# Five moves in one decoder layer: prompt compression inside the projection, and three out-projection blocks inside sample attention

## The chip, the cores and the metric

The kernel runs on one core of a Trainium2 chip. Its engines are TensorE (PE, with weight loads shown apart as PEld), VectorE (DVE), ScalarE (ACT), GpSimd (POOL) and SyncE (SP); each works through its own list of instructions, and semaphores tie the lists together. The metric is the device time of one execution in microseconds, as the median of several runs.

## The reference, cut to what matters

One layer of a hybrid decoder, in float32, for a prompt (1 x 512 rows) and a sample group (8 x 4 = 32 rows) that share every weight. All 544 rows stand side by side in the kernel.

```python
mod = silu(c) @ w_ada + b_ada; shift, scale, gate = split(mod, 3)
h = rms_norm(x, norm_g) * (1 + scale) + shift
(a_q, a_kv, a_gate, a_silu, b_in, b_silu, c_q, c_kv, c_iq, c_ik, c_iw, c_silu) = split_columns(h @ w_in)
# group A: for the rows so far, chunks of 32 positions, one every 16, become one key and one value:
#   hid = b1 + sum over 32 positions of (chunk + pe) @ w1 ;  gelu(hid) @ w2 + b2
#   o_a = gated sum of attention over compressed, selected and window keys (8 heads, 2 key heads)
# group B: trailing means of b_in, times pool_w ; group C: attention over keys that an indexer selects
mixed = concat(o_a * silu(a_silu), o_b * silu(b_silu), o_c * silu(c_silu))      # 2048 columns
y = x + gate * (mixed @ w_out)
```

The sample group attends to 2048 cached positions per sequence, read through a page table; the prompt group only to itself. A T5 bias table is added to all scores.

## The kernel before

The work runs in stages, which the windows of the trace below name by their time.

**0 to 484 us:** the cached rows of the sample group are compressed (16 groups of 16 pages, `NPOS` = 16; `load_rows`, `round_rows`, `turn_hid`, `w2_mm`), and beside that `mod` is computed. **484 to 525 us:** DVE's `modulate()` applies scale and shift to the normalised rows `hT` (16 feature blocks of 512 prompt rows, then the sample rows), the last group of the compression is finished, ACT and DVE round `h` into a high and a low part (`h_hi`, `h_lo`), and the first small jobs of the input projection begin in native float32. **To 1206 us:** the input projection. From job `J0` on there are 32 jobs, one for each block of 128 columns (called `jj` 0 to 31 here); each is 16 blocks `k` of the features times two halves of 272 rows times three products (low x high, high x low, high x high), so 96 matmuls. SP loads each job's weights in two pieces (`hw_raw`, `x` = 2 jj and 2 jj + 1), ACT and DVE round them (`hw_hi`, `hw_lo`). Other work hangs in this loop: `sample_indexer(j, k)` on PE, `hook(j)` on several engines.

**1206 to 1254 us (called phase 2 here):** the prompt's own compression. After the projection's last `silu` columns DVE adds the position embedding to the prompt's chunks (`xpe`), PE multiplies 2 x 32 of them by `w1P` (8 MB, loaded from 1205.7 us on), ACT applies gelu, PE `w2P`, and the keys `kcP` and values `vcP` come out. SP also loads here the bias of the prompt's scores (`bias`, 3 MB) and the rows of `silu` (`mix`, 4.35 MB), in one transfer each. **To 1430 us:** prompt attention, 48 units of one head and 128 rows; `scores(u)` on DVE adds the bias, `gated(u)` multiplies by `mix`, which thereby becomes `mixed`.

**1430 to 1701 us:** sample attention, in the steps head 0, body 0, head 1, turn 0, body 1, head 2, turn 1, body 2, turn 2. The 112 key blocks are numbered through: units 0 and 1 are the two key heads of group A (blocks 0 to 39 and 40 to 79), unit 2 is group C (80 to 111); head 1 has blocks 40 to 47, body 1 blocks 48 to 79, head 2 blocks 80 to 87, body 2 blocks 88 to 111. A block is loaded into one of `NKR` = 8 buffers `kn` (SP issues the loads of two of every four blocks, ACT the others, and each of them waits until the block eight before has been turned), turned by four PE transposes into bank 5 or 6 (`kb`), copied out by ACT (`kT`), and multiplied with the queries for four blocks at a time (`kmm`). In the bodies of units 1 and 2 the products of the unit before with its values stand among the blocks (`pv(u - 1, 0)` to `pv(u - 1, 5)`; 6 stands behind the body, 7 at the next turn; even numbers are the products, odd ones a small sum). POOL loads the values (`vr`, `vx`) page by page, into buffers that a `pv` has set free. A turn transposes the softmax's result. **1701 to 1919 us:** the out projection, 16 column blocks `nb` of 96 matmuls each (16 `k` x 2 halves x 3 products), then `y_turn(nb)`, five transposes back to rows; DVE scales by the gate and adds `x`; SP loads `wo`, ACT and DVE round it.

`after(engine, n)` is a barrier: it waits until all engines have ended phase n. PE's transposes and products in `kb`, `pv` and phase 2 are native float32, which PE runs as two records for each matmul; the rounded products are one record each.

Of the kernel before, what the change touches and what calls it, by code (L numbers as in the profile page):

```python
# [38 lines left out]
P = 128  # L39
# [20 lines left out]
NXP = KVH * NCP + 1  # L60
# [129 lines left out]
def build(nc, I, O):  # L190
# [3 lines left out]
    with ExitStack() as ctx:  # L194
# [94 lines left out]
        iqT = ext("iqT", P, 2 * TT)  # L289
        ikT = ext("ikT", P, T)  # L290
# [24 lines left out]
        w1p, w1pos = region(tp[0])  # L315
        w1P = [w1p(f"w1P{i}", P, 32 * 256) for i in range(2)]
        w1_early = (big_end - tp[0]) // (16 * 256 * 4)
        w2p, _ = region(w1pos[0])
        xpe = w2p("xpe", P, 2 * 32 * NXP)
        w2P = w2p("w2P", P, 2 * 2 * P)  # L320
        hidP = w2p("hidP", P, 4 * 64)
        cxP = w2p("cxP", P, 3 * 64)
        hidr = [w2p(f"hidr{i}", P, 256) for i in range(2)]
        att, apos = region(tp[0])
        bias = att("bias", P, 12 * T)
        assert 12 * T <= 32 * 256
# [7 lines left out]
        keep, _ = region(apos[0] + 12 * 1024)  # L334
        kc = keep("kc", P, DB * KVH * P)
# [134 lines left out]
        cr_x, cr_ps, cr_ev = sem("cr_x"), sem("cr_ps"), sem("cr_ev")  # L470
# [40 lines left out]
        mx_in = sem("mx_in")  # L511
# [22 lines left out]
        y_out = sem("y_out")  # L534
        BIAS_BANKS = (1, 4, 7, 1, 4)
# [131 lines left out]
        kb_gt, g_ = {}, 32  # L667
        for step, u in STEPS:
            if step == "turn":
                g_ += len(pgroups(u))  # L670
            else:
                for n in blocks_of(step, u):
                    kb_gt[n] = g_
                    g_ += 1

        by_act = [True] * 32
        for step, u in STEPS:
            if step == "turn":
                by_act += [(len(by_act) + i) % 2 == 0 for i in range(len(pgroups(u)))]
            else:  # L680
                by_act += [True] * len(blocks_of(step, u))
# [19 lines left out]
        def block_pages(eng, regs, b, first, n):  # L701

            eng.load(regs[0:n], ptab[0:1, b * NPG + first:b * NPG + first + n])
            return [eng.snap(regs[i], min_val=0, max_val=NPOOL - 1) for i in range(n)]

# [47 lines left out]
        def after(eng, n):  # L753

            eng.wait_ge(ph_pe, n)
            eng.wait_ge(ph_act, n)
            eng.wait_ge(ph_dve, n)
            if n == 4:
                eng.wait_ge(ph_pool, 1)
# [186 lines left out]
        def _(sp):  # L946
# [14 lines left out]
            def load_rows(g, first, n):  # L961
                kv, b = g // DB, g % DB
                if g >= 2:
                    sp.wait_ge(xn_tr, 8 * (g - 1))
                for x in range(first, first + n):
                    t, i = x // 4, x % 4
                    r = page(b, x)
                    sp.dma_start(xnat[(4 * g + t) % 8][32 * i:32 * i + 32, :].rearrange("p (l x) -> p l x", l=4),
                                 ca[bass.ds(r, 1), :, kv, :, :].rearrange("a (p l) h c -> (a p) l (h c)", l=4)).then_inc(xn_in[g % 2], 16)
# [12 lines left out]
            load_rows(0, 0, NPG)  # L982
            for i in range(2, 4):
                load_w1(0, i)
# [32 lines left out]
            for x in range(2 * (njobs - J0)):  # L1017
# [15 lines left out]
            for i in range(4):  # L1033
                if i == w1_early:
                    after(sp, 2)
                    for kv in range(2):
                        sp.dma_start(w2P[:, kv * 256:kv * 256 + 256].rearrange("p (n d) -> p n d", n=2), I["a_cmp_w2"][0, kv].rearrange("(n p) d -> p n d", p=P)).then_inc(late_in, 16)
                kv, s0 = i // 2, i % 2 * 16
                sp.dma_start(w1P[kv][:, s0 * 256:(s0 + 16) * 256].rearrange("p (s h) -> p s h", h=256),
                             I["a_cmp_w1"][0, kv].rearrange("(s p) h -> p s h", p=P)[:, s0:s0 + 16]).then_inc(w1q_in[i], 16)  # L1040

            for x in range(2):
                sp.wait_ge(sx_out[x], 16 * KD // 2)
            sp.dma_start(mix[:, :], d_mix).then_inc(mx_in, 16)

            sp.wait_ge(cr_ps, 1)
            sp.wait_ge(b_dma, 32 + 64)
            sp.dma_start(v3(bias, "p (h j) -> p h j", h=12), bass.AP(d_rep.tensor, d_rep.offset + 127, [[12 * TXL - 1, P], [TXL, 12], [1, T]])).then_inc(at_in, 16)
            after(sp, 3)
# [8 lines left out]
            after(sp, 4)  # L1058
            sw = I["state_a_win"][0]

            def keys(step, u):
                for n in blocks_of(step, u):
                    if n >= NKR:
                        if n % 4 >= 2:
                            continue
                        sp.wait_ge(kb_tr, kb_gt[n - NKR] + 1)
                    key_block(sp, regs, n)
# [19 lines left out]
            for c in range(D // CW):  # L1087
# [7 lines left out]
                elif c == 0:  # L1095
                    after(sp, 5)
# [6 lines left out]
        def _(pool):  # L1103
# [127 lines left out]
            after(pool, 4)  # L1231
# [12 lines left out]
        def _(pe):  # L1244
# [266 lines left out]
            def sample_indexer(j, k):  # L1511

                jj = j - J0
                if (jj, k) == (0, 1):
                    pe.wait_ge(a_free, aux)
                    pe.wait_ge(ixp_r, 12)
                    mm(bank[5][:, 0:4], expd[:, 2 * P:3 * P], iwS[:, :], start=True, stop=True).then_inc(si_ps, 1)
# [11 lines left out]
                if (jj, k) == (9, 11):  # L1529
                    ix_sum(4)  # L1530

# [18 lines left out]
            for j, (kind, b, t, c) in enumerate(jobs):  # L1550
                if free_need[j]:
                    pe.wait_ge(m_free, free_need[j])
                if j >= J0:
                    for k in range(KD):
# [5 lines left out]
                        sample_indexer(j, k)  # L1560
                        wh, wl = (v3(t_[x % 4], "p (k n) -> p k n", n=P)[:, k % 8, :] for t_ in (hw_hi, hw_lo))
# [14 lines left out]
                if c == SMALL:  # L1576
                    if j == 0:
                        pe.wait_ge(hw_in[0], in_need[0])
                    for k in range(KD):
                        if j == 0:  # L1580
                            pe.wait_ge(h_ready, k + 1)
                        if (j, k) == (0, 8):
                            turn_hid(15)
                        if (j, k) == (1, 8):
# [41 lines left out]
            pe.wait_ge(m_free, njobs)  # L1626
            for u in range(2):
                last = mm(bank[4][:, 24 * u:24 * u + 24], expd[:, u * P:(u + 1) * P], gateS0[:, :], start=True, stop=True)
            last.then_inc(pl_t, 1)
# [3 lines left out]
            after(pe, 2)  # L1633
            def turn_hidden(kv):
                pe.wait_ge(cr_ev, kv + 1)
                for hb in range(2):
                    tr(bank[2 + kv][:, 64 * hb:64 * hb + NXP], hidr[kv][0:NXP, hb * P:(hb + 1) * P], con[0:NXP, 0:NXP]).then_inc(cp_ps, 1)

            for kv in range(2):
                pe.wait_ge(cr_x, kv + 1)  # L1640
                for s in range(32):
                    if s % 16 == 0:
                        pe.wait_ge(w1q_in[2 * kv + s // 16], 48 + 16 * (2 * kv + s // 16 == 1))
                    last = mm(bank[kv][0:NXP, 0:256], xpe[:, (32 * kv + s) * NXP:(32 * kv + s + 1) * NXP], w1P[kv][:, s * 256:(s + 1) * 256],
                              start=(s == 0), stop=(s == 31))
                last.then_inc(cr_ps, 1)
            turn_hidden(0)
            turn_hidden(1)
            pe.wait_ge(late_in, 80)
            pe.wait_ge(cp_ev, 4)  # L1650
            for hb in range(2):
                last = mm(bank[4][:, 0:62], w2P[:, hb * P:(hb + 1) * P], hidP[:, hb * 64:hb * 64 + 62], start=(hb == 0), stop=(hb == 1))
            last.then_inc(cp_ps, 1)
            for h in range(KVH):
                for hb in range(2):
# [1229 lines left out]
```

## Time and profile before

| | us |
|---|---|
| median of 3 runs (smallest to largest) | 1922.06 (1920.43 to 1925.61) |
| the profiled execution | 1920.71 |
| its span | 1919.0 |
| PE busy (of the span) | 1731.9 (90%) |
| DVE busy | 1091.5 (57%) |
| ACT busy | 656.7 (34%) |

The chain that ended last runs through PE for 74% of the span; DVE has 7%, DMA 6%, SP's queue 5%. PE is the engine that sets the time in most stages, but not in all: in phase 2 and in sample attention it is idle for long stretches, which the windows below show.

### The profile page before, as it was taken

How to read it: one execution, taken by the hardware profiler on the slowest of the kernel's cores; microseconds unless marked ns; L12 is line 12 of the kernel's file. 1: busy time of each engine (PE TensorE's matmuls, PEld its weight loads, DVE VectorE, ACT ScalarE, POOL GpSimd, SP SyncE). 2: the span in 40 equal slices, each digit the busy share in tenths (PEclk: the TensorE clock that was granted, in tenths of full speed). 3: DMA queues.
4: the chain of work that ended last, by engine and by line, in shares of the span. 5: the costliest groups of instructions: out<-in, count | busy, mean ns of one | idle time of the engine just before them, and what ended most of it. 6: DMA issues, size and time to landing. Idle time of an engine off the chain costs nothing.

```text
span 1919.0 us, 34926 instructions
## 1 busy us (share of the span) xinstructions
PE 1731.9 (90%) x13423; PEld 1515.2 (79%) x13423; DVE 1091.5 (57%) x2145; ACT 656.7 (34%) x1339; POOL 224.2 (12%) x412
## 2 busy tenths in 40 slices
PE   5999989999799999999999999889976677769997
PEld 3788878989698888888999999567753444569997
DVE  4656685556434656344877746458765786343331
ACT  4555575555422312233222221044433333231110
POOL 1000000000001001432000000100012053710000
PEclk9999999999799989999999999859997788779999
DMA  9978868995323131655333332930018598753331
GB/s 237 259 209 229 242 175 232 288 261 167 89 72 107 62 106 45 174 176 171 106 83 83 102 90 68 320 122 2 1 58 259 165 289 243 215 181 96 119 123 47
DMA packets 275441, 291.39 MB, mean 152 GB/s; under 512 B 33093, under 2 KB 235318, under 8 KB 273597
## 3 DMA queue, kind: packets, MB, share of 16 engines
q1 hardware_dynamic: 233409, 210.82, 38.6%
q0 software_dynamic: 20000, 62.03, 9.8%
q10 hardware_dynamic: 21866, 16.30, 3.0%
q8 instruction: 107, 1.75, 0.4%
q14 instruction: 59, 0.48, 0.1%
HBM read 272.74 MB, written 29.14 MB: 157 GB/s over the span
## 4 chain that ended last, share of the span: by engine, by line
PE 74%; DVE 7%; DMA 6%; SPq 5%; issue 4%; ACT 3%; ACTq 1%; POOL 0%; POOLq 0%; DVEq 0%
PE bank L1564 6%; PE bank L1566 6%; PE bank L1565 6%; PE bank L1357 4%; PE bank L1356 4%; PE bank L1358 4%; PE bank L1898 3%; PE bank L1900 3%; PE bank L1899 3%; PE bank L1608 3%; PE bank L1609 3%; PE bank L1610 3%; PE bank L1334 3%; PE bank L1307 2%; DMA kn<-in_cache_a_kv_dram 2%
## 5 line engine op out<-in xcount | busy, mean ns | idle before, releaser
L1564 PE MATMUL bank<-h_lo,hw_hi 128*128 128x272 f32 x1024 | 305.2, 298 | 0.9 <-DVE hw_lo L2506 0.9
L1566 PE MATMUL bank<-h_hi,hw_hi 128*128 128x272 f32 x1024 | 296.7, 290 | 0.0
L1565 PE MATMUL bank<-h_hi,hw_lo 128*128 128x272 f32 x1024 | 295.3, 288 | 0.0
L1356 PE MATMUL bank<-w1hi,xl 128*128 128x256 f32 x768 | 225.5, 294 | 6.0 <-DVE w1lo L2332 3.8
L1357 PE MATMUL bank<-w1lo,xh 128*128 128x256 f32 x768 | 217.5, 283 | 0.0
L1358 PE MATMUL bank<-w1hi,xh 128*128 128x256 f32 x768 | 217.2, 283 | 0.0
L1564 PEld LDWEIGHTS bank<-h_lo,hw_hi 128*128 128x128 f32 x1024 | 193.2, 189 | 9.7 <-issue 9.0
L1565 PEld LDWEIGHTS bank<-h_hi,hw_lo 128*128 128x128 f32 x1024 | 193.6, 189 | 1.5 <-issue 1.0
L1566 PEld LDWEIGHTS bank<-h_hi,hw_hi 128*128 128x128 f32 x1024 | 193.2, 189 | 0.0
L2344 DVE TENSOR_TENSOR xd<-bank,xd 128x256 f32<-128x256 f32 (+1 forms) x256 | 90.3, 415 | 141.7 <-ACT xd L1970 141.2
L1898 PE MATMUL bank<-mix_lo,wo_hi 128*128 128x272 f32 x512 | 150.4, 294 | 5.8 <-DVE mix_lo L2824 5.8
L2506 DVE TENSOR_TENSOR hw_lo<-hw_raw,hw_hi 128x1024 fp32r<-128x1024 f32 x64 | 78.2, 1222 | 133.5 <-ACT hw_hi L2105 116.9
L1356 PEld LDWEIGHTS bank<-w1hi,xl 128*128 128x128 f32 x768 | 147.2, 192 | 8.5 <-issue 7.2
L1900 PE MATMUL bank<-mix_hi,wo_hi 128*128 128x272 f32 x512 | 149.0, 291 | 0.0
L1899 PE MATMUL bank<-mix_hi,wo_lo 128*128 128x272 f32 x512 | 148.2, 289 | 0.0
L1357 PEld LDWEIGHTS bank<-w1lo,xh 128*128 128x128 f32 x768 | 147.4, 192 | 0.4
L1358 PEld LDWEIGHTS bank<-w1hi,xh 128*128 128x128 f32 x768 | 147.1, 192 | 0.0
L1608 PE MATMUL bank<-pw_hi,h_lo 128*128 128x256 f32 x448 | 132.0, 295 | 0.0
L1609 PE MATMUL bank<-pw_lo,h_hi 128*128 128x256 f32 x448 | 129.0, 288 | 0.0
L1610 PE MATMUL bank<-pw_hi,h_hi 128*128 128x256 f32 x448 | 128.2, 286 | 0.0
L2349 DVE TENSOR_TENSOR xl<-xd,xh 128x512 fp32r<-128x512 f32 (+1 forms) x192 | 120.8, 684 | 2.2
L1975 ACT CAST xh<-xd 128x512 fp32r<-128x512 f32 (+1 forms) x192 | 113.7, 619 | 16.9 <-DVE xd L2344 14.2
(424 smaller groups left out, 3561.4 us busy)
## 6 DMA issues: line engine op xcount, KB each, us to landing
wa<-in_w_ada_dram SPq DMA_DIRECT2D x48, 1024.0 KB, 7.6
xnat<-in_cache_a_kv_dram SPq DMA_DIRECT2D x256, 128.0 KB, 7.0
hw_raw<-in_w_in_dram SPq DMA_DIRECT2D x64, 512.0 KB, 4.0
pw_raw<-in_w_in_dram SPq DMA_DIRECT2D x16, 1024.0 KB, 6.7
vr<-in_cache_a_kv_dram POOLq DMA_DIRECT2D x128, 128.0 KB, 5.7
wo<-in_w_out_dram SPq DMA_DIRECT2D x8, 2048.0 KB, 11.7
w1P<-in_a_cmp_w_dram SPq DMA_DIRECT2D x4, 2048.0 KB, 12.2
kn<-in_cache_a_kv_dram ACTq DMA_DIRECT2D x64, 128.0 KB, 4.0
```

Of the source, the lines that this page charges most:

```text
L1356: mm(o, lo, wh, start=at, stop=False, skip_group_check=True)
L1357: mm(o, hi, wl, start=False, stop=False, skip_group_check=True)
L1358: last = mm(o, hi, wh, start=False, stop=end, skip_group_check=True)
L1564: mm(o, wh, hl[:, k, tc], start=(k == 0), stop=False)
L1565: mm(o, wl, hh[:, k, tc], start=False, stop=False)
L1566: last = mm(o, wh, hh[:, k, tc], start=False, stop=(k == KD - 1))
L1608: mm(o, hl[:, k, tc], wh, start=(k == 0), stop=False)
L1609: mm(o, hh[:, k, tc], wl, start=False, stop=False)
L1610: last = mm(o, hh[:, k, tc], wh, start=False, stop=(k == KD - 1))
L1898: mm(o, wh[:, k, :], ml[:, k, cols], start=(k == 0), stop=False)
L1899: mm(o, wl[:, k, :], mh[:, k, cols], start=False, stop=False)
L1900: last = mm(o, wh[:, k, :], mh[:, k, cols], start=False, stop=(k == KD - 1))
```

## The change

Seven edits stand in the diff; all serve the same output.

1. Start: ACT issues the second half of the first group's page loads (8 of 16), SP the first half and then three of the four weight pieces `w1S` (before, ACT issued one piece more and SP all 16 pages).
2. `modulate()`: DVE scales the even feature blocks, ACT the odd ones, and the call moves behind the compression's last group; PE's `turn_hid(15)` and `w2_mm(15)` move from (job 0, k 8) and (job 1, k 8) to (0, 6) and (1, 2).
3. The sample gate's small matmuls move from phase 2 into job jj 0, and its exps and reciprocals into jj 20 and 22.
4. Phase 2 is gone: the prompt's compression is done inside the projection, without the adds of the position embedding (its product is known from the sample's compression and is added as the bias `b1e`). Eight pairs of 16 matmuls stand in jobs jj 10 to 13, each on a 32-column tile of the array, four tiles with different weights at a time. Their weights `w1c` (8 MB, in pairs of 512 KB) are loaded by SP between the `hw_raw`. Transposes, `w2P` and the norm follow in jj 14 to 19.
5. `bias` is loaded in four pieces and `mix` in three, right after the last projection job; scores and `gated` wait for the piece they read.
6. In sample attention, `early_out` computes column blocks 13, 14 and 15 of the out projection for the 512 prompt rows, in native float32: 4 pieces for each block, a piece being 16 matmuls of 128 columns into the bank that the key blocks use, and a copy by ACT into `yE`. The pieces stand behind blocks 10, 14, 18 and 22 of body 1, 2, 4, 6 and 8 of head 2, and 9, 13, 17 and 21 of body 2. SP loads `wE` (1 MB) three times. The eight `pv` all stand inside the body now, one every four (body 1) or three (body 2) blocks.
7. In the out projection, blocks 13 to 15 then have 48 matmuls of 32 columns (the sample rows) in place of 96 of 272.

```diff
+            def prompt_blocks(jj, k):
...
+                    for s in range(4):
+                        for kv in range(2):
+                            for h in range(KVH):
+                                q, tap = 2 * kv + h, 4 * pr + s
+                                last = mm(bank[6][32 * q:32 * q + NCP, 0:256], cmp4[:, kv, h, tap:tap + 16 * (NCP - 1) + 1:16],
+                                          w1c[2 * (pr % 2) + kv][:, s * 256:(s + 1) * 256], start=(tap == 0), stop=(tap == 31), tile_position=(0, 32 * q))
...
+                if x in (16, 20, 24, 25, 26, 27, 28, 29):
+                    pr = (16, 20, 24, 25, 26, 27, 28, 29).index(x)
+                    if pr < 2:
+                        sp.wait_ge(kb_tr, 24 + 8 * pr)
+                    else:
+                        sp.wait_ge(cr_ps, pr - 1)
...
             sp.wait_ge(m_done, njobs)
...
+                if i == 0:
+                    sp.dma_start(mix3[:, 0:8, :], dm[:, 0:8, :]).then_inc(mx_in, 16)
+            sp.dma_start(mix3[:, 12:16, :], dm[:, 12:16, :]).then_inc(mxc_in, 16)
...
+            def early_out(i, x):
...
+                kturn(gt)
+                for k in range(KD):
+                    last = mm(bank[5 + gt % 2][:, 0:P], wE[:, k * P:(k + 1) * P], mix3[:, k, x * P:(x + 1) * P], start=(k == 0), stop=(k == KD - 1))
...
-                every = len(ns) // 6
+                every = len(ns) // 8
...
+                    if (step, u, y) in piece_at:
+                        early_out(*piece_at[(step, u, y)])
...
-                if step == "body" and u >= 1:
-                    pv(u - 1, 6)
...
+                if nb in EARLY_NB:
+                    o, cols = bank[2 * (nb % 2) + 1][:, T - HALF:HALF], slice(T, TT)
```

The order of PE's instructions at two places follows (a matmul is written output, then stationary or moving operand and the other; `x16` is sixteen alike in a row).

PE between the projection and prompt attention, before (`kcP,aqT` is the first product of prompt attention):

```order
L1628 MATMUL bank<-gateS_58,expd 128x24 x2
L1644 MATMUL bank<-w1P_136,xpe 63x256 x32
L1644 MATMUL bank<-w1P_137,xpe 63x256 x32
L1637 MATMUL bank<-con,hidr_142 128x63 x2
L1637 MATMUL bank<-con,hidr_143 128x63 x2
L1652 MATMUL bank<-hidP,w2P 128x62 x2
L1656 MATMUL bank<-w2P,hidP 31x128 x4
L1660 MATMUL bank<-cxP,con 128x62
L1674 MATMUL bank<-kcP,aqT 128x7
```

The whole compression stood alone here. The same place on PE now (`bT` and `wk` are the last transposes of the projection):

```order
L1685 MATMUL bank<-con,bT 16x128
L1686 MATMUL bank<-con,wk 32x128
L1704 MATMUL bank<-kcP,aqT 128x7
L1705 MATMUL bank<-kslcT,aqT 128x128
L1706 MATMUL bank<-kwinT,aqT 128x128
```

The scores follow the projection directly. The first pair on PE now, in job jj 10 (`h,hw` are the projection's products; the two `w1c` rows come four times in a pair):

```order
L1627 MATMUL bank<-h_lo,hw_hi_103 128x272
L1628 MATMUL bank<-h_hi,hw_lo_99 128x272
L1629 MATMUL bank<-h_hi,hw_hi_103 128x272
L1570 MATMUL bank<-w1c_140,cmpT 31x256 x2
L1570 MATMUL bank<-w1c_141,cmpT 31x256 x2
```

The 64 matmuls with 63 weight columns have become 128 with 31, eight lots of 16 among the projection's.

PE in body 1, before (`kn` is a key block, `kT,zq` its product with the queries, `opart` an odd `pv`):

```order
L1755 MATMUL bank<-kT_244,zq 32x256
L1784 MATMUL bank<-con,opart 128x16 x2
L1743 MATMUL bank<-con,kn_153 128x128 x4
L1743 MATMUL bank<-con,kn_154 128x128 x4
L1743 MATMUL bank<-con,kn_155 128x128 x4
L1848 MATMUL bank<-sC,con 128x127
L1743 MATMUL bank<-con,kn_156 128x128 x4
```

Here PE has nothing but key blocks and small sums. The same body on PE now, at a piece of column block 13 (`vN`, `vc` and `win_v` begin an even `pv`):

```order
L1789 MATMUL bank<-kT_248,zq 32x256
L1807 MATMUL bank<-mix,wE 128x128 x16
L1777 MATMUL bank<-con,kn_153 128x128 x4
L1777 MATMUL bank<-con,kn_154 128x128 x4
L1818 MATMUL bank<-vN,pT 32x256 x2
L1818 MATMUL bank<-vc,pT 32x256
L1818 MATMUL bank<-win_v,pT 32x256 x4
```

Between two key blocks stand 16 more matmuls with full weights, and an even `pv` comes every eight blocks in place of every ten.

## Rows read from the trace of the kernel before

**Rows 1.** Windows by stage: bounds, length, busy us (records), PE clock, DMA share, GB/s
```profile
484.40:525.00 40.60, 27.50 (x192) 26.02 (x192) 17.48 (x47) 16.07 (x31) 2.17 (x4) 0.71 0.29 90
525.00:1205.70 680.70, 661.95 (x5186) 624.78 (x5187) 401.35 (x556) 172.85 (x328) 75.64 (x141) 0.99 0.35 103
1205.70:1254.20 48.50, 34.88 (x162) 22.18 (x162) 18.17 (x39) 6.12 (x15) 5.08 (x10) 0.87 0.97 344
1527.80:1580.30 52.50, 41.69 (x414) 25.75 (x416) 44.01 (x50) 20.22 (x39) 25.83 (x48) 0.90 0.91 280
1580.30:1608.20 27.90, 20.55 (x122) 11.83 (x122) 11.96 (x26) 8.69 (x15) 9.38 (x16) 0.71 0.79 229
1608.20:1647.10 38.90, 31.90 (x298) 18.10 (x300) 29.56 (x20) 14.22 (x27) 21.09 (x38) 0.96 0.79 236
1647.10:1701.10 54.00, 32.18 (x356) 21.97 (x356) 12.26 (x28) 11.01 (x21) 31.98 (x59) 0.57 0.69 204
1701.10:1907.00 205.90, 205.23 (x1611) 203.55 (x1611) 69.13 (x105) 33.46 (x26) 9.20 (x14) 0.99 0.33 107
```

**Rows 2.** Timeline, projection's end to the first scores: start, length, instruction [idle before]
```profile
1211.40 0.91 DVE L2631 SCALAR_TENSOR_TENSOR rs<-bank,vecT,rs 128x272 f32<-128x272 f32 x2
...
1256.00 0.17 DVE L2295 CUSTOM_DVE_ANT_0 SP<-bank,bias 128x7 f32<-128x7 f32 x1 [1.97 <-PE bank L1676]
```

**Rows 3.** DMA issues: transfer, queue, count, KB each, median us to landing
```profile
hw_raw<-in_w_in_dram SPq DMA_DIRECT2D x64, 512.0 KB, 4.0
w1P<-in_a_cmp_w_dram SPq DMA_DIRECT2D x4, 2048.0 KB, 12.2
bias<-bias_repeated SPq DMA_DIRECT2D x1, 3072.0 KB, 19.7
```

**Rows 4.** Matmuls that stand nearest to the moved ones in shape; the first is a group
```profile
L1644 PE MATMUL bank<-w1P,xpe 128*63 128x256 f32 x128 | 29.4, 394 | 4.6 <-DVE xpe L2657 4.6
249.15 1.07 PE L1321 MATMUL bank<-w1S,peT 128*32 128x256 f32 x16 [0.62 <-DMA w1S<-in_a_cmp_w_dram]
518.03 1.46 PE L1545 MATMUL bank<-pw_raw,hs 128*32 128x92 f32 x32
519.41 1.80 PE L1588 MATMUL bank<-pw_raw,hT 128*128 128x92 f32 x7
```

**Rows 5.** Timeline of the modulation and of what follows it
```profile
484.42 7.39 DVE L2355 TENSOR_SCALAR hT<-hT,ascale,modT 128x512 f32<-128x512 f32 x16 [0.18 <-ACT hT L1983]
504.73 0.42 DVE L2408 TENSOR_TENSOR kcb<-bank,gk 127x256 f32<-127x256 f32 x1 [9.68 <-PE bank L1387]
505.32 4.48 ACT L1933 CAST h_hi<-hT 128x544 fp32r<-128x544 f32 x8 [7.89 <-DVEq L2292]
```

**Rows 6.** Timeline of the start: SP's page loads and PE's first use
```profile
5.47 13.64 SPq L968 DMA_DIRECT2D xnat<-in_cache_a_kv_dram  x16
28.13 1.97 PE L1334 MATMUL bank<-con,xnat 128*128 128x128 f32 x8 [7.89 <-DMA xnat<-in_cache_a_kv_dram]
```

**Rows 7.** PE with full weights, one instruction at both clocks, a wait of sample attention's end
```profile
1426.74 2.00 PE L1713 MATMUL bank<-PTP,cvnat 128*128 128x128 f32 x16
PE bank L1771 <- DMA vx<-in_cache_c_kv_dram: 9.8, 3, 4.8
1582.52 4.04 PE L1771 MATMUL bank<-vr,pT 128*32 128x256 f32 x29
1648.27 2.10 PE L1771 MATMUL bank<-vr,pT 128*32 128x256 f32 x29
```

**Rows 8.** Out projection: the turns of two blocks, a matmul with few columns, rounding groups
```profile
1723.09 0.60 PE L1883 MATMUL bank<-con,yT 128*128 128x128 f32 x4
1735.67 0.60 PE L1883 MATMUL bank<-con,yT 128*128 128x128 f32 x4
96.66 1.06 PE L1289 MATMUL bank<-con,mpart 128*128 128x9 f32 x8
L2824 DVE TENSOR_TENSOR wo_lo<-wo,wo_hi 128x2048 fp32r<-128x2048 f32 x15 | 34.1, 2282 | 9.6 <-ACT wo_hi L2282 9.6
```

More of the change, by code:

```diff
@@ L313, in build @@
         prw = tmp("prw", TS, 1024)
[L315 to L323, printed above, removed]
+        pq, _ = region(iq_at)
+        hidr = pq("hidr", P, 256)
+        hidP = pq("hidP", P, 4 * 64)
+        cxP = pq("cxP", P, 3 * 64)
+        w2P = sb("w2P", P, 2 * 2 * P, at=ik_at)
+        assert 256 + 256 + 192 <= 2 * TT and 512 <= T
+        w1c = [sb(f"w1c{i}", P, 4 * 256, at=base_free + 4096 * i) for i in range(4)]
         att, apos = region(tp[0])
         bias = att("bias", P, 12 * T)
-        assert 12 * T <= 32 * 256
         SP_ = [att(f"SP{i}", P, 1056) for i in range(3)]
@@ L334, in build @@
         keep, _ = region(apos[0] + 12 * 1024)
+        wE = sb("wE", P, KD * P, at=apos[0] + 12 * 1024)
+        yE = [sb(f"yE{i}", P, TT, at=mask_at + 4 * TT * i) for i in range(3)]
+        assert DB * KVH == KD and 3 * TT <= 256 + 384 + 512 + 4 * P
         kc = keep("kc", P, DB * KVH * P)
@@ L981, in _ @@
             sp.wait_ge(w1q_in[1], 16)
-            load_rows(0, 0, NPG)
-            for i in range(2, 4):
+            load_rows(0, 0, NPG // 2)
+            for i in range(1, 4):
                 load_w1(0, i)
@@ L1516, in sample_indexer @@
                     pe.wait_ge(ixp_r, 12)
+                    for u in range(2):
+                        mm(bank[4][:, 24 * u:24 * u + 24], expd[:, u * P:(u + 1) * P], gateS0[:, :], start=True, stop=True)
                     mm(bank[5][:, 0:4], expd[:, 2 * P:3 * P], iwS[:, :], start=True, stop=True).then_inc(si_ps, 1)
@@ L1624, in _ @@
             last.then_inc(pl_t, 1)
[L1626 to L1629, printed above, removed]
             end_phase()
[L1633 to L1655, printed above, removed]
[L1656 to L1664 removed]
+            pe.wait_ge(m_free, njobs - 1)
+            pe.wait_ge(a_free, aux)
+            pe.wait_ge(pl_c, 1)
             def qk(u):
@@ L2023, in _ @@
                 if p == NPOS:
-                    act.wait_ge(h_ready, KD + 4)
+                    act.wait_ge(m_mod, 1)
+                    act.wait_ge(x_ev, 4 * (QT + 1))
+                    for k in range(1, KD, 2):
+                        A(hT3[:, k, 0:T], hT3[:, k, 0:T], ACT.Identity, scale=asc3[:, k, 0:1], bias=mod3[:, k, 0:1]).then_inc(x_ev, 1)
+                    act.wait_ge(h_ready, KD // 2 + 4)
                     act.copy(v3(hs, "p (k t) -> p k t", t=TS), hT3[:, :, T:TT]).then_inc(hh_a, 1)
```

300 lines of the change are left out of this document (177 added, 123 removed).

## The prediction

> **What bounds the kernel now.** I read the windows by stage first, then the timeline where one stage hands over to the next, then the prices of the shapes that move. In the projection and the out projection PE is busy for 97% and nearly 100% of the time at full clock (661.95 of 680.70 us, 205.23 of 205.90) [rows 1]: there every PE instruction added costs its own time, and every one removed gives it back. In phase 2 the window shows something else: PE 34.88 of 48.50 us, and no other engine more than 18 us; what runs is one chain of PE, ACT and DVE, while DMA is full (0.97). In sample attention PE has 41.69 of 52.50 us in body 1 and 31.90 of 38.90 in body 2; behind body 2 it has 32.18 of 54.00 at a clock of 0.57 [rows 1]. So work that moves out of phase 2 into the projection turns chain time into PE time, and work that moves from the out projection into sample attention may fill gaps there. The question is how much of it fills and how much lengthens.
>
> **Start.** SP issued 16 page loads in 13.64 us, 0.85 each, and PE sat idle for 7.89 us before the first group at 28.13 [rows 6]. With half issued by ACT, the last is issued up to 6.8 us sooner. The other end is 0, if transfers and not issuing set the landing. I take -3, the middle, since the trace doesn't separate the two. By the Trainium skill ("DMA: Bandwidth & Descriptors", "Issuing engines are not separate DMA queues") a second issuing engine saves only the sequencer's time, which it calls usually small beside the transfer; here the issuing is 13.64 us [rows 6], not small, so by the rule the gain would be up to the 6.8 us and by its "usually small" near 0, and the sum would move by 3 to 4 us either way.
>
> **Modulation.** DVE's 16 operations took 7.39 us from 484.42 to 491.81; the last group's key block `kcb` came out at 504.73, and ACT began to round `h` at 505.32, behind the barrier that waits for it [rows 5]. Now DVE finishes the last group's sum before it modulates, so that the chain to `kcb` starts about 7.39 us sooner, and PE's two spots on that chain move up by 4 of the 16 feature blocks between them, a quarter of a tail that was 12.9 us at most (504.73 - 491.81): 3.2 at best. ACT takes over 8 operations, so `h` itself is ready 3.7 us sooner. The ends are -10.6 and -3.7; I take -8, since both chains start sooner and the later one decides.
>
> **Prompt compression.** Removed: DVE's last operation on the projection's columns ended at 1211.40 + 0.91 = 1212.31, and the first scores came at 1256.00 [rows 2]. Now nothing stands between: PE's first products of the attention need only ACT's copies out of two banks, so the first scores should start at about 1212.6, if the first quarter of `bias` has landed. That quarter (768 KB) is issued as the projection ends; the whole took 19.7 us for 3072 KB among other transfers, so a quarter takes about 5 (estimate) and lands near 1211; if it took all the 19.7, 13 us would come back [rows 3]. Gain 43.4, at worst 30. Added to a PE that is already full: 128 matmuls of 256 columns on 32-column tiles. Nearest is the position embedding's product, the same shape but for a weight column, where 16 records, 8 matmuls, took 1.07 us: 0.134 each, 17.1 in all. The low end is the 92-column form, 16 matmuls from 518.03 to 519.41, 0.086 each, 11; the high end is what one matmul costs when tiles don't overlap, phase 2's own 29.4 us for 64: 0.46 each, 58.8 [rows 4]. I take 17.1, because columns and tiling are those of its row. Transposes, `w2P`, the norm and the gate's products are some 22 records; full matmuls on raw weights took 1.80 us for 7 [rows 4], 5.7 at that price; I take 3, as most are narrower. ACT's and DVE's small operations lie beside PE, which waits for none of them: each result has at least half a job (6 us) before PE reads it. Sum: -43.4 + 17.1 + 3 = -23.3, with ends of -29 and +18.
>
> Sixteen such tile products already stand between full-width ones in the first jobs: from their start at 518.03 to that of the next group at 519.41 are 1.38 us, and no gap shows [rows 4]. The Trainium skill ("TensorEngine Tiling (Array Packing)", "Key Properties") says that a change of tiling mode drains the array: by it each of the 16 changes would cost something, and the sum would be a few us worse.
>
> SP's loads for the pairs stand among those for the projection. For six of the eight, the load is issued 15/16 of a job before PE reads it, some 11.8 us when a job is as long as a block of the out projection, which has the same 96 matmuls (1735.67 - 1723.09 = 12.58 [rows 8]). Three transfers of 512 KB lie in that queue; one took 4.0 us, and 2048 KB took 12.2 [rows 3]. So they land in about 9 (estimate), with 2 or 3 us to spare. The loads of `hw_raw` behind them have two jobs of slack.
>
> **Sample attention.** Eight full-weight matmuls of 128 columns took 2.00 us in 16 records, so a piece of 16 takes at most 4.0 at full clock; at half clock, by one instruction seen at both (4.04 and 2.10 us for 29 records), 7.7 [rows 7]. Twelve pieces are 48 us of PE at full clock. An even `pv` is 23 matmuls, 46 records, 3.3 us warm and 6.4 cold by the same rows; one more of them lies inside each body now. Stage by stage [rows 1]:
> Body 1 has 41.69 busy in 52.50. With 16.0 and 3.8 more (piece and `pv` with its sum) it would be 61.5 if every gap were filled, 72.3 if none were. Busy time counts modelled ends, so it is rather too high; a tenth less would give 55 to 57. I take +7.5; the ends are +2.5 and +19.8. DMA isn't the limit: 0.91 of 52.5 us plus 1 MB at 280 GB/s, 3.7 us, is 51.5.
> Head 2 and turn 1 lose the cold `pv(0, 6)` and gain four pieces: 20.55 - 6.4 - 1 + 16 = 29.2 if gaps are filled, against 27.90. I take +1; the ends are -2 and +9.6. The softmax chain of unit 1 (before, all that ran here) lies under the pieces.
> Body 2 has 31.90 in 38.90; with 19.8 more, 51.7 filled, 58.7 not. I take +13; ends +11 and +20.
> Behind body 2, PE waited 9.8 us for value pages [rows 7]. POOL can load them only into buffers that a `pv` of unit 1 has freed, and these `pv` now come well before the body's end. What is late next is the softmax of unit 2 and eight products at half clock. I take -8; ends -9.8 and 0.
> Sum: 7.5 + 1 + 13 - 8 = +13.5, ends of about +2 and +49.
>
> **Out projection.** A block takes 12.58, of which five turns 0.55: 12.03 for 96 matmuls, 0.125 each. A short block has 48 matmuls with the same weights and 32 columns. Eight records with 9 columns took 1.06, 0.133 each; without the last one's end they are nearer 0.11 [rows 8]. So 5.3 to 6.4 us for 48, saving 5.6 to 6.7 a block. I take 19 for three, ends 17 and 20. Rounding hides under it: DVE's `wo_lo` takes 2.28 us a block [rows 8].
>
> **Sum.** -3 - 8 - 23.3 + 13.5 - 19 = -39.8. The profiled execution took 1920.71 us, so 1880.9; the median of the runs shown is 1.35 above it, which gives 1882.
>
> **Rivals.**
> *The gaps of sample attention don't fill.* Pieces then lengthen every step, at the extreme with the ends above (+49): 1917. Halfway, 1900. For it: PE waits there for copies and loads that come no sooner, a piece delays the next key block's transposes, and the load of `wE` stands in SP's queue ahead of two key blocks. Against it: a piece needs nothing that the key blocks wait for, and while it runs, ACT copies and loads land.
> *They fill better*, with busy time overstated and the tail at its end: +2 in place of +13.5, 1870, with a little from the start 1866.
> *The column tiles don't overlap* between products of another kind: 58.8 in place of 17.1, 1924, no change. Against it speak both tile rows.
> *The pairs wait for their weights.* This ends slower. If the 1.5 MB in SP's queue took as long as `bias` did (19.7 us [rows 3]), each of six pairs would wait 19.7 - 11.8 = 7.9, 47 in all: 1930. It decides from 19.4 us of landing on. Against it: DMA is busy for 0.35 of the projection [rows 1], while `bias` landed among full engines.
>
> **How the numbers follow.** A measurement of this kernel can tell about 0.3%, 5.8 us, from no change. The forecast, 1872 to 1894, has 0.72; unfilled gaps 0.14, nearly all still faster; better filled 0.08; tiles that don't overlap 0.03; late weights 0.03. Faster 0.92, no change 0.04, slower 0.04. The range runs from 1864 to 1906; outside are the two last rivals, half of the better case and a third of the worse.
>
> **What would show it.** Right: the first scores within 2 us of DVE's last `rs` operation; each pair between two projection products in about 2.1 us with no DMA wait; body 1 near 60, body 2 near 52 us; short blocks of about 6 us. Wrong: waits of PE for `w1c` or for the first `bias` quarter; matmul pairs of 4 us and more; a clock below 0.9 in body 1 or 2; pieces followed by the same waits for `kT` and `kn` as before; value pages that still end the chain behind body 2.

## The result, and the profile after

The changed kernel took 1897.22 us as the median of four runs (1893.94 to 1901.19), beside 1921.24 for the kernel before in the same lot: a ratio of 0.989, with a 95% interval of 0.987 to 0.992. The forecast was 1882 with a range of 1864 to 1906. So the sign and the range held, but of the 40 us that were expected about 24 came. The profiled execution (1901.19 us, span 1899.5) lies 4 us above that median, and its span is 19.5 us shorter than before.

The windows by stage, in the columns of [rows 1]: the projection's 32 jobs, the passage to the first scores, body 1 with the wait behind it, head 2 with turn 1, body 2, what follows it, the full blocks of the out projection and its last two short blocks.

```profile
758.80:1214.80 456.00, 449.40 (x3614) 427.98 (x3615) 276.39 (x308) 120.31 (x194) 52.54 (x98) 1.00 0.46 131
1214.80:1222.10 7.30, 2.98 (x21) 2.18 (x19) 5.71 (x7) 1.74 (x4) 0.10 (x1) 0.91 0.88 301
...
1493.30:1565.10 71.80, 58.44 (x590) 41.53 (x590) 48.37 (x56) 21.73 (x44) 34.34 (x64) 0.91 0.86 264
1565.10:1594.70 29.60, 26.87 (x199) 22.22 (x199) 6.87 (x14) 9.42 (x18) 0.00 (x0) 0.94 0.50 146
1594.70:1647.70 53.00, 48.82 (x473) 33.78 (x473) 30.25 (x28) 16.11 (x32) 31.06 (x59) 1.00 0.84 244
1647.70:1690.70 43.00, 26.64 (x308) 19.10 (x308) 12.30 (x28) 10.79 (x21) 20.91 (x38) 0.58 0.65 195
1690.70:1851.40 160.70, 160.70 (x1256) 159.10 (x1257) 59.30 (x87) 32.08 (x26) 6.56 (x10) 0.99 0.39 126
...
1863.80:1887.50 23.70, 23.70 (x113) 23.51 (x114) 3.51 (x10) 0.00 (x0) 1.31 (x2) 0.50 0.10 34
```

Read from top to bottom, phase 2's 48.5 us have shrunk to 7.3, and body 1, 52.5 before, stands at 71.8 with the wait behind it. The last row holds the surprise: PE is busy all the time, but the granted clock is 0.50, half of full speed. Between the same marks of the two traces (when `h` begins to be rounded, the projection's last product, the first scores, prompt attention's last product, the first out-projection product, the end) the differences in us are:

| stretch | before | after | change | forecast |
|---|---|---|---|---|
| start to the rounding of `h` | 505.3 | 497.8 | -7.5 | -11 |
| to the projection's last product | 700.1 | 717.0 | +16.9 | +20.1 |
| to the first scores | 50.6 | 7.3 | -43.3 | -43.4 |
| prompt attention | 172.5 | 170.7 | -1.7 | 0 |
| sample attention | 272.7 | 297.9 | +25.2 | +13.5 |
| out projection | 217.9 | 208.8 | -9.1 | -19 |

These are two single executions. Sample attention, the same code in three of the kernels below, took 303.5, 290.8 and 291.3 us there, so its +25.2 is one of +18.1, +18.6, +25.2 and +30.8.

The compression did what was worked out. On the timeline of the changed kernel, DVE's last operation on the projection's columns and the first scores, as in [rows 2]:

```profile
1220.80 0.91 DVE L2721 SCALAR_TENSOR_TENSOR rs<-bank,vecT,rs 128x272 f32<-128x272 f32 x2
...
1222.09 0.17 DVE L2363 CUSTOM_DVE_ANT_0 SP<-bank,bias 128x7 f32<-128x7 f32 x1 [0.38 <-DVEq L2360]
```

The scores start 0.38 us behind; no wait for the `bias` quarter shows. And the first pair inside the projection, on PE:

```profile
918.14 0.29 PE L1629 MATMUL bank<-h_hi,hw_hi 128*128 128x272 f32 x1
918.36 1.96 PE L1570 MATMUL bank<-w1c,cmpT 128*31 128x256 f32 x32
920.25 0.39 PE L1627 MATMUL bank<-h_lo,hw_hi 128*128 128x272 f32 x1
```

From the pair's start to that of the next projection product are 1.89 us for 16 matmuls, 0.118 each, and no idle time for its weights stands ahead of it; the other seven pairs lie between 1.89 and 1.90. The step into the pair takes 0.22 in place of 0.12, and the first product behind it stands 0.23 ahead of the second, so a change of tiling costs about 0.1 us each way, 1.6 for all 16.

The modulation, as in [rows 5]:

```profile
487.83 3.73 DVE L2423 TENSOR_SCALAR hT<-hT,ascale,modT 128x512 f32<-128x512 f32 x8
...
488.71 5.75 ACT L2082 ACTIVATE hT<-hT,modT,ascale 128x512 f32<-128x512 f32 x8
...
497.24 0.42 DVE L2478 TENSOR_TENSOR kcb<-bank,gk 127x256 f32<-127x256 f32 x1 [3.56 <-PE bank L1410]
...
497.82 1.74 ACT L1988 CAST h_hi<-hT 128x544 fp32r<-128x544 f32 x3 [1.83 <-DVEq L2360]
```

From its first operation to the rounding of `h` it takes 9.99 us where it took 20.90. It begins 3.4 us later than before, 1.1 of them because the last group's sum now stands ahead of it; the rest is no more than profiles differ by (483.0 to 489.0 us in the ten kernels here with the new modulation). The start, as in [rows 6]:

```profile
5.36 8.14 SPq L714 DMA_DIRECT2D xnat<-in_cache_a_kv_dram  x8
5.37 8.30 ACTq L714 DMA_DIRECT2D xnat<-in_cache_a_kv_dram  x8
13.54 11.20 SPq L970 DMA_DIRECT2D w1S<-in_a_cmp_w_dram  x3
24.79 4.39 SPq L993 DMA_DIRECT2D w2S<-in_a_cmp_w_dram  x2
26.00 1.57 PEld L1357 LDWEIGHTS bank<-con,xnat 128*128 128x128 f32 x8 [5.78 <-DMA xnat<-in_cache_a_kv_dram]
...
30.40 2.09 SPq L714 DMA_DIRECT2D xnat<-in_cache_a_kv_dram  x3
```

The first group came 2.1 us sooner, but SP was then held for 11.2 us by three weight pieces, and the second group's pages went out at 30.40, no sooner than the 29.99 of before.

### The profile page after: what moved, and what is told of

The parts are those of the page before. It is cut to its first block, busy times and chain, and to the rows that moved or that the text cites. A ratio compares the mean times of both kernels' runs of the same rounds, so it can differ in the third digit from the quotient of the medians.

```text
span 1899.5 us, 35676 instructions
## 1 busy us (share of the span) xinstructions
PE 1738.7 (92%) x13789; PEld 1532.0 (81%) x13789; DVE 1077.8 (57%) x2122; ACT 666.9 (35%) x1361; POOL 221.8 (12%) x412
## 3 DMA queue, kind: packets, MB, share of 16 engines
q1 hardware_dynamic: 244625, 213.97, 39.8%
## 4 chain that ended last, share of the span: by engine, by line
PE 77%; DVE 7%; DMA 6%; SPq 4%; ACT 3%; issue 2%; ACTq 1%; POOL 0%; DVEq 0%; POOLq 0%
PE bank L1627 6%; PE bank L1629 6%; PE bank L1628 6%; PE bank L1379 4%; PE bank L1380 4%; PE bank L1381 4%; PE bank L1671 3%; PE bank L1951 3%; PE bank L1953 3%; PE bank L1672 3%; PE bank L1673 3%; PE bank L1952 3%; PE bank L1357 3%; PE bank L1330 2%; PE bank L1807 2%
## 5 line engine op out<-in xcount | busy, mean ns | idle before, releaser
L1951 PE MATMUL bank<-mix_lo,wo_hi 128*128 128x272 f32 x416 | 122.5, 294 | 5.8 <-DVE mix_lo L2877 5.8
L1953 PE MATMUL bank<-mix_hi,wo_hi 128*128 128x272 f32 x416 | 121.1, 291 | 0.0
L1952 PE MATMUL bank<-mix_hi,wo_lo 128*128 128x272 f32 x416 | 120.5, 290 | 0.0
```

The costliest lines, as they stand in the source:

```text
L1951: mm(o, wh[:, k, :], ml[:, k, cols], start=(k == 0), stop=False)
L1952: mm(o, wl[:, k, :], mh[:, k, cols], start=False, stop=False)
L1953: last = mm(o, wh[:, k, :], mh[:, k, cols], start=False, stop=(k == KD - 1))
```

## The experiments

All ran on the chip beside the kernel before; ratios are to that kernel, with a 95% interval. A lot of four or two shares a chip.

**The changed kernel once more.** No edit.

> The changed kernel itself, unaltered, so that the other kernels of this lot have it beside them on the same chip. From its first runs: 0.989 of the kernel before (1897 us against 1921).

It took 1895.75 us, 0.987 (0.983 to 0.990). This is the mark for the runs on top of the changed kernel.

**Without early blocks.**

```diff
-        EARLY_NB = (13, 14, 15)
+        EARLY_NB = ()
...
+        EARLY_LOAD = {}
...
+        piece_at = {}
```

> The changed kernel without early column blocks: no pieces and no wE loads in sample attention, and all 16 column blocks of the out projection at full width; the eight pv keep their new places. Theory (the stages of the two traces, where sample attention became 25 us longer and the out projection only 9 us shorter): the early blocks cost more than they give, so this kernel is faster than the changed one, by up to 16 us, some 1881 to 1887 us, ratio to before 0.979 to 0.982. Rival (the prediction's own terms, pieces and pv together +13.5, short blocks -19): it is about 5 us slower than the changed kernel, near 1902 us, 0.990 to 0.993.

1873.22 us, 0.975 (0.972 to 0.978): 22.5 us faster than the changed kernel in the same lot, more than the theory had, and the rival had the wrong sign. The early blocks are a loss. Its windows for body 1, head 2 with turn 1, body 2, and what follows:

```profile
1488.40:1541.90 53.50, 42.65 (x462) 27.00 (x463) 43.93 (x50) 20.51 (x40) 34.49 (x64) 0.94 0.92 289
1541.90:1565.30 23.40, 15.58 (x73) 9.73 (x73) 11.33 (x20) 8.51 (x14) 0.03 (x1) 0.62 0.87 243
1565.30:1606.00 40.70, 34.65 (x346) 19.30 (x346) 30.18 (x27) 14.78 (x28) 25.74 (x48) 1.00 0.93 267
1606.00:1652.30 46.30, 21.91 (x307) 15.96 (x308) 12.26 (x28) 10.75 (x20) 26.22 (x48) 0.63 0.69 203
```

Against the changed kernel's windows that is 18.3 less in body 1 and the wait behind it, 6.2 in head 2, 12.3 in body 2 and 3.3 more behind it (there PE waits 8 us for value pages): 33 us for twelve pieces, while the short blocks give back 9. With the other profiles of both codes the pieces cost between 26 and 40. It also shows what the new places of the `pv` are worth by themselves: from prompt attention's end to the out projection this kernel takes 265.1 us, two more kernels without early blocks 263.5 and 264.0, the kernel before 272.7.

**Short blocks at full width.**

```diff
-                    o, cols = bank[2 * (nb % 2) + 1][:, T - HALF:HALF], slice(T, TT)
+                    o, cols = bank[2 * (nb % 2) + 1][:, 0:HALF], slice(HALF, TT)
```

> One line of the changed kernel: the 48 matmuls of each of the three short blocks multiply 272 columns (the second half of all rows, of which only the last 32 are used) in place of 32. Theory (the clock falls while only 32 columns stream: the short blocks ran at 0.2135 us a matmul where full ones take 0.125): with 272 columns the clock stays, a short block takes about 6.5 in place of 11.2 us, and the kernel becomes 12 to 14 us faster although it computes more: 1884 us, ratio 0.982. Rival (a matmul with other operands costs 0.21 us whatever the clock, or the clock falls for another reason): 11 us and more for a block, no gain or slower, 0.989 and above.

1886.85 us, 0.983 (0.980 to 0.986): 8.9 faster than the changed kernel, with more work. In the changed kernel, two matmuls of the first short block and two of the second:

```profile
1858.05 0.26 PE L1942 MATMUL bank<-mix_hi,wo_hi 128*128 128x32 f32 x1
1858.16 0.26 PE L1940 MATMUL bank<-mix_lo,wo_hi 128*128 128x32 f32 x1
...
1866.11 0.37 PE L1940 MATMUL bank<-mix_lo,wo_hi 128*128 128x32 f32 x1
1866.32 0.37 PE L1941 MATMUL bank<-mix_hi,wo_lo 128*128 128x32 f32 x1
```

They stand 0.11 apart at first and 0.21 later, with the same shapes. With 272 columns, the window from the turn of block 12 to that of block 14:

```profile
1855.50:1868.60 13.10, 13.10 (x108) 13.08 (x107) 2.84 (x8) 0.00 (x0) 1.31 (x2) 1.00 0.15 53
```

Two short blocks take 13.1 us at a clock of 1.00, where the changed kernel took 22.4 at 0.50. The edit changes nothing but the columns and where they land in the bank, so the theory holds: the clock fell because nothing but 32-column matmuls streamed, though PE was busy without a gap. In all six profiles with three 32-column blocks the last two took 11.2 us each. The gain is two blocks' worth and not three, since the first short block had kept most of its clock (0.89). Even so this kernel stays 14 us above the one without early blocks.

**The start as before.**

```diff
-            load_rows(0, 0, NPG // 2)
-            for i in range(1, 4):
+            load_rows(0, 0, NPG)
+            for i in range(2, 4):
...
-            for x in range(NPG // 2, NPG):
-                row_page(act, page, 0, x)
+            act.dma_start(w1S[1][:, 0:8 * 256].rearrange("p (u h) -> p u h", h=256), w1[0][1]).then_inc(w1q_in[1], 16)
```

> The changed kernel with the start of the kernel before: ACT issues the second weight piece, SP all 16 page loads of the first group. Theory (in the trace of the changed kernel the first group came 2.1 us sooner, but the second group's pages later, and modulation began 3.4 us later, 1.3 of them for the sum that now stands ahead of it): the new start gives nothing, so this kernel is as fast as the changed one or up to 3 us faster, 0.988 to 0.990. Rival (the prediction): it is 3 us slower, 0.991.

1893.36 us, 0.986 (0.983 to 0.989), 2.4 below the changed kernel's 1895.75, inside both intervals. To see less than that, the same edit was tried on the faster kernel:

> The kernel without early blocks and with the start of the kernel before. Theory (spreading the first group's loads gives nothing): within 2 us of the kernel without early blocks, ratio 0.974 to 0.976. Rival (the prediction): 3 us slower, 0.9765.

1873.08 us, 0.977 (0.975 to 0.980), beside 1873.22 in the earlier lot. Together: the new start gives nothing that these runs can tell, and 3 us either way can't be excluded. The first group itself did come sooner, at 25.4 to 27.8 us in every profile with the new start, at 28.1 to 29.8 in the three with the old.

**One load of `wE`.** The loads for blocks 14 and 15 are left out.

```diff
                             if i == 0:
                                 sp.wait_ge(un_ps, 3)
-                            else:
-                                sp.wait_ge(kb_tr, out_gt[(i - 1, QT - 1)] + 1)
-                            nb = EARLY_NB[i]
...
+                                nb = EARLY_NB[i]
...
-                    pe.wait_ge(mxc_in, 16 + 16 * (i + 1))
+                    pe.wait_ge(mxc_in, 32)
```

> The changed kernel with one load of wE in place of three; the pieces of blocks 14 and 15 then multiply with the weights of block 13, so that those columns of the prompt's output are left out. Theory (the pieces cost their own PE time, loads only the waits that the trace shows at block 80, 4.6 us, and shortly before, 1.8): 5 to 7 us faster than the changed kernel, ratio to before 0.983 to 0.985. Rival (the megabyte ahead of the key blocks' loads is what costs): most of the 33 us that the early blocks add to sample attention goes, 15 us faster and more, 0.980 or less.

**Half of each piece.**

```diff
-                for k in range(KD):
...
+                for k in range(KD // 2):
...
```

> The changed kernel with 8 of the 16 products in each piece (half of the sum over features is left out for the prompt rows of the three early blocks); loads, banks, copies and waits are as before. 12 pieces lose 22 us of PE time. Theory (a piece costs its PE time, of which only a quarter falls into gaps: 44 us of pieces lengthened the stage by 33): 15 to 18 us faster than the changed kernel, ratio 0.978 to 0.980. Rival (what costs is the hand-over: the bank that key blocks use too, ACT's wait and copy, the loads): 8 us faster at most, 0.983 and above.

One load: 1893.45 us, 0.987 (0.984 to 0.990), no gain that can be told; the rival's 15 us are out, the theory's 5 are just not. Half pieces: 1887.49, 0.984 (0.982 to 0.987), 8 us for 22 us of PE time, as its rival had it. By these times neither PE's time nor the loads alone set the cost. That led to the next.

**Both cuts.**

> Both of the last cuts at once: 8 of 16 products in each piece and one load of wE, so that half of the sum, and the right weights for blocks 14 and 15, are left out for the prompt rows. One load alone gave nothing to speak of (0.987), half pieces alone about 8 us (0.984), and in body 1 the half pieces' trace has the DMA engines at 0.97 of the stage. Theory (body 1 has two limits of nearly the same height, PE with the pieces and DMA with wE, so that taking one away uncovers the other): together they give more than the sum of both, 15 us and more under the changed kernel, 0.980 or less. Rival (the cuts simply add up, and the rest is the hand-over of twelve pieces): 0.982 to 0.984.

1878.22 us, 0.977 (0.974 to 0.981): 17.5 us under the changed kernel, where the sum of the two cuts is 10.6. That is 7 us beyond the sum, 14 if the ratios are taken, and the intervals of the four runs leave such a difference uncertain by some 12. So that the cuts do more together than alone is likely, but not shown.

The theory was about body 1, and there the traces don't bear it out. Body 1 with one load, with half pieces, with both, and unaltered in the kernel with wide short blocks, in the columns of [rows 1]:

```profile
1490.10:1555.80 65.70, 58.26 (x591) 41.38 (x591) 44.01 (x50) 21.73 (x44) 33.71 (x63) 0.95 0.82 255
```
```profile
1483.00:1546.50 63.50, 50.87 (x527) 34.73 (x527) 47.76 (x56) 21.62 (x44) 34.34 (x64) 0.91 0.97 296
```
```profile
1493.10:1550.10 57.00, 49.28 (x526) 33.40 (x527) 43.98 (x50) 21.62 (x44) 33.00 (x62) 0.98 0.94 291
```
```profile
1493.10:1558.00 64.90, 56.84 (x590) 40.67 (x590) 43.97 (x50) 21.63 (x44) 34.27 (x64) 0.96 0.87 268
```

From 71.8 us the single cuts take 6.1 and 8.3, both 14.8, about their sum. And 71.8 is only one of four profiles of the same body 1. In each, the stretch can be split into PE's busy time, its wait for block 80 at the end, and the rest of its idle time:

| kernel | body 1 | PE busy | wait for block 80 | other idle time |
|---|---|---|---|---|
| changed | 71.8 | 58.4 | 4.6 | 8.8 |
| changed, once more | 72.2 | 58.4 | 5.1 | 8.7 |
| start as before | 66.3 | 58.0 | 0.5 | 7.8 |
| wide short blocks | 64.9 | 56.8 | 0 | 8.1 |
| one load | 65.7 | 58.3 | 0 | 7.4 |
| half pieces | 63.5 | 50.9 | 3.9 | 8.7 |
| both | 57.0 | 49.3 | 0 | 7.7 |
| no early blocks | 53.5 | 42.7 | 0 | 10.8 |

So half pieces make body 1 shorter by about the PE time that they take away, with one load as with three. One load takes away nothing but the wait for block 80, and two of the four kernels with three loads had next to none of it. DMA, at 0.82 to 0.97 in these windows, may set the length once the pieces are halved; where they are whole it doesn't: at 0.82 body 1 was no shorter than at 0.87.

**One block in PE's waits.** On the kernel without early blocks, block 13 alone.

```diff
+        EARLY_NB = (13,)
+        EARLY_LOAD = {FIRSTB[2] + 16: 0}
+        piece_at = {('body', 2, 25): (0, 0), ('body', 2, 26): (0, 1), ('turn', 2, 5): (0, 2), ('turn', 2, 6): (0, 3)}
...
```

(25 and 26 stand behind the body's 24 blocks; the other two behind the sixth and seventh of unit 2's eight products.)

> The kernel without early blocks (0.975), with one early block (13) back, whose four pieces stand where PE was seen waiting: two behind body 2, under the softmax of unit 2 (9.1 us), two behind the sixth and seventh of the last eight products, under the value loads (8 us in two waits). Its short block stands alone between full ones. Theory (a piece is free only where PE waits, and one short block alone keeps the clock): it saves the 6 us of the short block and costs 1 to 2, so 4 to 5 us faster than without early blocks, ratio 0.972 to 0.973. Rival (the pieces delay the last chain, or the load of wE the value loads): as fast or slower, 0.975 and above.

1872.31 us, 0.976 (0.973 to 0.979), beside 0.975: no difference that can be told. The out projection became 5.3 us shorter (212.7 for 218.0), where 6 were expected, and two pieces filled the softmax's wait: PE, at body 2's end,

```profile
1607.20 7.39 PE L1817 MATMUL bank<-mix,wE 128*128 128x128 f32 x64
1616.48 3.84 PE L1876 MATMUL bank<-con,sS 128*128 128x128 f32 x17 [1.88 <-DVE sS L934]
...
1629.42 1.94 PE L1828 MATMUL bank<-vr,pT 128*32 128x128 f32 x32
...
1637.67 5.17 PE L1817 MATMUL bank<-mix,wE 128*128 128x128 f32 x32
...
1644.36 3.82 PE L1817 MATMUL bank<-mix,wE 128*128 128x128 f32 x32
```

The wait of 9.1 has become 1.88 and turn 2 starts on time. But from there to the out projection it took 39.7 us, 2.7 more than without, though the kernel without early blocks waits 8 us for value pages here. Most of the products with those pages ran at half clock (1.94 us), where that kernel had most of them at full clock:

```profile
1627.47 1.08 PE L1818 MATMUL bank<-vr,pT 128*32 128x128 f32 x32
```

The slow clock alone costs nothing here, and it needn't be of this edit's making. The kernel of the next experiment has the same code in this stage as the one without early blocks; it ran these products at half clock too, waited only 1.19 us for the pages, and took 36.2 us:

```profile
1638.35 1.94 PE L1818 MATMUL bank<-vr,pT 128*32 128x128 f32 x32
...
1650.91 0.60 PE L1818 MATMUL bank<-cvN,pT 32*32 32x128 f32 x2 [1.19 <-DMA vx<-in_cache_c_kv_dram]
```

So at half clock little was left of the wait that the last two pieces, 9 us of PE together, were to fill: from the end of the sixth product to the out projection this kernel took 18.5 us, that one 13.5. Why the clock is low in some executions and not in others isn't settled. Stretches that the edit doesn't touch differ by several us between the profiles, so the rest of the balance isn't told by them.

**The modulation as before,** on the kernel without early blocks:

```diff
-                        if (j, k) == (0, 6):
+                        if (j, k) == (0, 8):
...
-                for k in range(0, KD, 2):
+                for k in range(KD):
...
-                if p == NPOS:
-                    modulate()
...
+                if p == NPOS - 1:
+                    modulate()
```

> The kernel without early blocks and with the modulation of the kernel before (all 16 blocks on DVE, ahead of the last group's sum, and PE's two spots back at their old places). Theory (the traces have the rounding of h 7 to 9 us sooner with the new modulation): 7 to 9 us slower than without early blocks, ratio 0.979 to 0.981. Rival (the gain is given back in the first small jobs): no difference, 0.975.

1883.66 us, 0.981 (0.978 to 0.983) beside 0.975 (0.972 to 0.978): the new modulation is worth about 10 us, by the intervals somewhere between 4 and 19. The key block and the rounding of `h`, here:

```profile
502.42 0.42 DVE L2472 TENSOR_TENSOR kcb<-bank,gk 127x256 f32<-127x256 f32 x1 [9.75 <-PE bank L1410]
503.01 2.28 ACT L1988 CAST h_hi<-hT 128x544 fp32r<-128x544 f32 x4 [7.97 <-DVEq L2356]
```

In the kernel with the new modulation ACT's rounding starts at 495.48, with the modulation's start within a microsecond of this one. From its first operation to the rounding, the new modulation took 10.0 to 12.5 us in ten profiles, the old one 20.9 and 21.0.

No experiment undid the compression's move: its terms are read from the traces alone. In all eleven profiles of kernels with it the gap to the first scores is 7.3 us and a pair takes 1.89 to 1.90; the whole projection grew by 12.9 to 21.5.

## Why the prediction was right or wrong, point by point

**Start, -3 forecast: nothing that the runs can tell.** The step that failed is that the first group's landing would carry through. It was sooner by 2.1 us, but the second group's pages, which SP issues behind the weights, were not. Issuing was moved, not removed: what ACT took over from SP, SP spent on weights.

**Modulation, -8: right.** About 10 us by the run that undoes it, 8.4 to 11 by the traces from its first operation on; that -8 was too small isn't shown. Both chains did start sooner, and the later one decided.

**Compression, -43.4 + 17.1 + 3: right.** The gap to the first scores is 7.3 against 50.6, a gain of 43.3. A pair costs 1.89 where 2.1 was taken, eight are 15.1, and the projection grew by 16.9 in all in this profile. The tiles overlap, also between products of another kind, and no pair waits for weights, so both of those rivals are out. The quarter of `bias` came in time.

**Sample attention, +13.5: mis-sized, +25.2.** Here lie 12 of the 20 us by which the profiled execution missed the forecast; the other three profiles of this code have +18.1 to +30.8, so the term is too small in each. By its own parts:

| part | forecast | measured |
|---|---|---|
| up to block 48 | 0 | +1.1 |
| body 1 (52.5 us) | +7.5 | +14.8 (67.3 us) |
| head 2 and turn 1 (27.9) | +1 | +6.3 (34.2, of which 4.6 is a wait for block 80) |
| body 2 (38.6) | +13 | +14.4 |
| behind it (54.3) | -8 | -11.4 |

Body 2 and the end held. The step that failed in body 1 is that the pieces would fill its gaps. What PE waited for there (in us, times, longest), first before (1527.8 to 1586.6 us), then with the pieces (1493.0 to 1565.2):

```profile
PE bank L1743 <- ACT kT L846: 5.3, 10, 1.3
PE bank L1743 <- DMA kn<-in_cache_a_kv_dram: 2.8, 2, 2.6
PE bank L1755 <- ACT kT L846: 2.6, 1, 2.6
```
```profile
PE bank L1777 <- DMA kn<-in_cache_c_kv_dram: 4.6, 1, 4.6
PE bank L1777 <- DMA kn<-in_cache_a_kv_dram: 3.4, 2, 1.8
PE bank L1777 <- ACT kT L857: 2.7, 4, 0.9
PE bank L1789 <- ACT kT L857: 2.5, 1, 2.5
```

Before, PE waited 7.9 us for ACT's copies of key blocks and 2.8 for their loads; with the pieces, still 5.2 and 3.4. Its busy time rose by 16.7 us (58.4 for 41.7), its idle time without the last wait fell by 2 (8.8 for 10.8), where the forecast of 60 us left only 3 to 5. That the same waits for `kT` and `kn` remain is the sign of being wrong that the prediction itself had named; its rival of unfilled gaps, given 0.14, is what came here.

The other part is the first row, 4.6 us for block 80. The second load of `wE` was not counted in body 1. It stands in SP's queue ahead of block 80's own load: SP took 10 us to issue the first eight page loads behind it, 4.4 in the kernel with one load. How long PE then waits is partly luck (0 to 5.1 us in the four profiles of this code).

The sentence that DMA isn't the limit, 0.91 of 52.5 us plus 3.7 for a megabyte, had the price of a load right. The queue that carries `wE` (packets, MB, share of the 16 engines), in body 1 without early blocks and with them:

```profile
q1 hardware_dynamic: 5577, 4.12, 25.7%
```
```profile
q1 hardware_dynamic: 9805, 6.31, 30.2%
```

Over 53.5 and 71.8 us that is 13.7 and 21.7 us of all engines, 7.9 for two loads, so about 4 each.

**Out projection, -19: mis-sized, -9.1.** The price of a short block, 5.3 to 6.4 us, is right for the first one, which took 5.9. The other two took 11.2 each, because the granted clock fell to 0.50. The step that failed is to price a matmul by its record at full clock and to let the clock stand, when the change alters what streams through the array. I had weighed the clock for sample attention, and not here, in the one stage where PE never waits.

**The sum.** The forecast's -39.8 and the profile's -19.5 differ by 20: 11.7 from sample attention, 9.9 from the out projection, 3.5 from the start and the modulation's later beginning, less 3.2 and 1.7 from the projection and prompt attention. The medians differ by less, 24 against 40, since the profiled execution of the changed kernel lies 4 us above its median. That the result fell within 1864 to 1906 is owed to the width of the range: two terms missed by about 10 us each, both to the slow side. The best version here is the changed kernel without edits 6 and 7's early blocks, but with the `pv` in their new places: 1873 us, 0.975.

## What to carry to other kernels

An engine that looks idle is only room if the new work takes the place of a wait. Here PE waited for the copies of its own key blocks, and those waits stayed when more work was put between them; so list what ends the idle time first, and ask of each wait whether it would be gone. Add up also what the new work brings into the queues that the stage already uses: a load ahead of a critical one can cost more by its place than by its size. Before a stage's length is read as the effect of an edit, look at that stage in kernels in which its code is the same: here one body took 64.9 to 72.2 us, as much as the cuts that were to explain it. And when matmuls are made narrower, the time of one at full clock isn't its price until a trace shows that the clock holds: here 272 columns were cheaper than 32.

## What the runs showed of the hardware that was not expected

PE busy for 23.70 of 23.70 us was granted a clock of 0.50 (the 1.2 GHz level) while only 32-column matmuls with full weights streamed; the 5.9 us before, with the first such block, had 0.89, and with 272 columns in the same place it had 1.00. The same code was granted different clocks in different executions: at the end of sample attention a product with the value pages took 1.08 us in one profile and 1.94 in another, with granted clocks of 1.00 and 0.50 around it. Four matmuls on 32-column tiles of the array with four different weights kept their overlap between full-width products, at 0.118 us a matmul, and the steps into them and out of them took about 0.1 us more each than one between full-width products.
